# Two empty steps in the context lane of the gate/up stage, and its first step ahead of the weave

## The chip, the cores and the metric

One core of a Trainium2 chip runs the kernel. Its engines work side by side, each through a list of instructions in order: TensorE (PE: products and transposes), VectorE (DVE), ScalarE (ACT), GpSimd (POOL), and SyncE (SP), which only issues loads. They wait for each other on semaphores. The metric is the time of one execution on the chip, in microseconds, as the median of several runs.

## The reference

The kernel computes two blocks of a transformer in a row on `x` (256 tokens of 1024), in float32. The first block is a hybrid attention mixer followed by a gated feed-forward. The second is a gated linear attention (GLA) and retention mixer, started from states that a context of 256 further tokens yields, followed by experts that choose their tokens. Cut to what the changed loop computes:

```python
def _swiglu(h, w_gate_up, w_down):
    gate, up = jnp.split(h @ w_gate_up, 2, axis=-1)      # 22 weight slots
    return (jax.nn.silu(gate) * up) @ w_down

hc = _rmsnorm(ctx, norm1_w[i]) * (1.0 + mod_c[1]) + mod_c[0]
def _context_states(hc, w_in, gla_gate_w, gla_gate_b, ret_decay_logit):
    _, gk, gv, log_a, _, _, rk, rv, _ = _project(hc, w_in, gla_gate_w, gla_gate_b, None)
    # log_a = log_sigmoid(z @ gla_gate_w + gla_gate_b) / 16
    log_gamma = jax.nn.log_sigmoid(ret_decay_logit.astype(F32))
    s_gf = _gla_final_state(gk, gv, log_a[:, :, 0])      # k * exp(b_end - b), then k^T v
    s_gb = _gla_final_state(_flip(gk), _flip(gv), _flip(log_a[:, :, 1]))
    s_rf = _ret_final_state(rk, rv, log_gamma[0])
    s_rb = _ret_final_state(_flip(rk), _flip(rv), log_gamma[1])
    return (s_gf, s_gb, s_rf, s_rb)
```

The feed-forward of the first block (gate/up, then down) and the context's states of the second do not depend on each other.

## The kernel before

All activations stay on the chip; the weights come as slots of 128 x 2048 numbers (1 MB) into a ring, in the order of the list `ORDER`, and `sync` issues a slot's load when the last user of its place is done. A dense product (`dense`, L656 to L658) runs at reduced precision in three passes per weight tile, with weights and activations split in a high and a low part. ScalarE copies a slot to its high part (`top_half`, L2404), VectorE subtracts for the low part (`low`, L1490), then TensorE makes 24 products over both token tiles; ScalarE and VectorE prepare slot n+2 while TensorE is at slot n.

The stage of the change is the gate/up product. It is woven from three lanes, Python generators of which each `yield` ends a step:

- "g" (`ffn` in each engine, 23 steps): slot n of gate/up. A group of 256 features is complete after two slots; then ScalarE takes a tanh (L2597), VectorE forms the gated product (L1367, called for it in its `ffn`), and with the next even slot TensorE transposes it (`gated_T`, L565 through `tr`), behind that slot's products. ScalarE copies the transposes out (L2587) ahead of its next copy of a slot.
- "c" (`context` in each engine, 22 steps): first the setup: ScalarE issues the loads of the context and its gates' weights, and a small log-sigmoid of 8 numbers per row is taken (VectorE L1367, ScalarE L2603 and L2605, VectorE L1367). Then the context's norm: squares (L2363), reciprocal root on GpSimd (L2857, L2859), scaling by VectorE (L1453) and ScalarE (L2365), eight tiles transposed by TensorE in four steps (L565) and copied out with scale and shift (L1463, L2375). Then three projection slots (`proj`, L957), the gates' narrow product z (L967), `pre` (L975), the log-sigmoid of 128 x 1024 (L1943, L1367, ScalarE L2603, L2605, VectorE L1367, L1946), decay products (L987, L989) with exp (L2640) and key scaling (L1952), state products (L1001), projection slots 3 to 6, scaling of the retention keys (L1972, L1977), and the last state products in two pairs (L1020), of which each bank is copied out (L1984 by VectorE, L2653 by ScalarE) before it is used again.
- "f" (VectorE alone, 20 steps): half a slot of the modulation weights each (`vads`, L1409).

`schedules` makes one list of letters, `FFN`, that TensorE, VectorE, ScalarE and the order of the loads go through alike: at a letter, an engine runs the next step of that lane (an engine that has no "f" skips it). No lane's step is tied to another's by the weave here: it takes "g f c f" in turn until each lane is used up:

```python
n = {"g": 23, "c": 22, "f": 2 * len(UNITS_FFN)}
ffn = weave(dict.fromkeys(n, 0), n, {}, "gcf", "gfcf")
```

So c_k stands behind g_k, all through. An engine's own list is rigid: where an instruction waits, all behind it wait. The list also orders the loads: a gate/up slot at each "g", the slots of the context's weights at given steps of "c". Before the loop stands the end of the attention block (`post`, `norm_scaled`, L635); behind it the down projection, whose first two slots are prepared by ScalarE and VectorE in the steps g_20 and g_21.

Of the kernel before, what the change touches and what calls it, by code (L numbers as in the profile page):

```python
# [52 lines left out]
def weave(done, counts, needs, main, turns):  # L53

    out = []
    while any(done[k] < counts[k] for k in main):
        for k in turns:
            if done[k] < counts[k] and all(done[a] >= n for a, n in needs.get((k, done[k]), ())):
                out.append(k)
                done[k] += 1  # L60
    return out


def schedules():

    n = {"p": 3, "f": 16, "0": 18, "1": 18, "i": 24, "d": 7, "c": 14, "o": 7}
    done = dict.fromkeys(n, 0)
    att = weave(done, n, {}, "p", "pf")
    needs = {}
    for h in "01":  # L70
        for t in range(2):
            needs[h, 12 + 3 * t] = [("d", 7), ("i", 12 * (t + 1))]
    for t in range(2):
        needs["c", 9 + 4 * t] = [("0", 3 * t + 3), ("1", 3 * t + 3)]
    for k in range(2):
        needs["o", k] = [("i", 12)]
    needs["o", 2] = [("0", 12), ("1", 12), ("c", 14), ("i", 21)]
    att += weave(done, n, needs, "0i1dco", "icf0i1do")
    att += "f" * (n["f"] - done["f"])
    n = {"g": 23, "c": 22, "f": 2 * len(UNITS_FFN)}  # L80
    ffn = weave(dict.fromkeys(n, 0), n, {}, "gcf", "gfcf")
    return att, ffn


# [1 line left out]
UNITS_IN1, UNITS_OUT1, UNITS_FFN, UNITS_DN = list(range(8, 18)), [18, 19], [20, 21, 22, 23] + list(range(32, 38)), list(range(38, 48))  # L86
# [85 lines left out]
class Book:  # L172
# [11 lines left out]
    def sig(self, name, *index):  # L184
        engine, lane, *event = name.split()
        key = f"{engine}_{lane}"
        if key not in self.sems:
            self.sems[key] = self.make(f"s_{key}")
        n = self.count[key] = self.count.get(key, 0) + 1
        if event:  # L190
            if self.dry:
                assert (name, *index) not in self.value, (name, index)
                self.value[(name, *index)] = n
            assert self.value[(name, *index)] == n, (name, index)
        self.latest[engine] = (self.sems[key], n)
        return self.sems[key], 1
# [48 lines left out]
def build(nc, D, out, coff):  # L245

    ctx = ExitStack()
    with ctx:
# [38 lines left out]
        def two(v):  # L287
            return v.rearrange("p (t d) -> p t d", t=2)
# [149 lines left out]
        seen = {"f": 0, "c": 0, "u": 0, "g": 0}  # L438
# [12 lines left out]
        for k in FFN:  # L451
            if k == "g" and seen["g"] < len(PLAN["gu"]):
                want_dense("gu", seen["g"])
            if k == "c" and seen["c"] in (6, 7, 8, 15, 16, 17, 18):
                i = (6, 7, 8, 15, 16, 17, 18).index(seen["c"])
                g, k0, kk = PLAN_CTX[i]
                n = kk * G_CTX[g][1]
                want("ctx", i, D["w_ctx"][i][:, 0:n], n)
            if k == "f" and seen["f"] % 2 == 0:
                want_vad(UNITS_FFN[seen["f"] // 2])  # L460
            seen[k] += 1
# [97 lines left out]
        def tensor(e):  # L559
# [38 lines left out]

            def norm(S, junk, banks, free):

                yield
                for k in range(0, 8, 2):
                    b = banks[k // 2 % len(banks)]
                    w.wait_ge(*at(f"v {S} x0"))
                    w.wait_ge(*at(f"a {S} x1"))
                    for f in free(k):
                        w.wait_ge(*f)
                    for j in (k, k + 1):
                        for t in range(2):
                            i = tr(PS[:, b, 256 * (j % 2) + 128 * t:256 * (j % 2) + 128 * t + 128], two(junk)[:, t, 128 * j:128 * j + 128])  # L610
                    i.then_inc(*sig(f"pe {S} tr", k))
                    yield
# [324 lines left out]
            def context():  # L937
# [28 lines left out]
                for k in range(8):  # L966
                    i = mm(PS[0:32, 7, 0:256], GZW[:, k, :], hcv[:, k, :], start=k == 0, stop=k == 7)  # L967
# [4 lines left out]
                for t in range(2):  # L972
                    if t:
                        w.wait_ge(*at("v ctx ev", 1))
                    mm(PS[:, 7 - t, :], GZc[0:32, 128 * t:128 * t + 128], GWc[0:32, :], start=True, stop=True).then_inc(*sig("pe ctx pre", t))  # L975
                yield
                L, KW = two(CX[:, 0:1024]), CX[:, 1024:2048].rearrange("p (d t n) -> p d t n", d=2, t=2)
                for d in range(2):
                    for t in range(2):
# [7 lines left out]
                        i = mm(PS[:, b, 0:256], C("gt") if d == 0 else C("lt"), L[:, t, 256 * d:256 * d + 256], start=True, stop=not far)  # L987
                        if far:
                            i = mm(PS[:, b, 0:256], C("ones"), L[:, 1 - t, 256 * d:256 * d + 256], start=False, stop=True)  # L989
                        i.then_inc(*sig("pe ctx kw", d, t))  # L990
                    yield
                for d in range(2):
                    for r in range(2):
# [6 lines left out]
                        for t in range(2):  # L1000
                            i = mm(PS[:, 7 - r, 0:256], KW[:, d, t, 128 * r:128 * r + 128], pcv[:, t, 256 + 256 * r:512 + 256 * r], start=t == 0, stop=t == 1)  # L1001
# [297 lines left out]
            n = 0  # L1299
# [62 lines left out]
        def vector(e):  # L1362
# [87 lines left out]
            def norm(S, src, junk, st, banks, aff, dst, mine=(2, 6)):  # L1450

                w.wait_ge(*at(f"g {S} rs"))
                ts(two(junk)[:, 0, :], src[:, 0, :], st[:, 2:3], None, ALU.mult).then_inc(*sig(f"v {S} x0"))  # L1453
                yield
                for k in range(0, 8, 2):
                    if k in mine:
                        b = banks[k // 2 % len(banks)]
                        w.wait_ge(*at(f"pe {S} tr", k))
                        if aff is None:
                            cp(dst[:, 256 * k:256 * k + 512], PS[:, b, :]).then_inc(*sig(f"v {S} h", k))  # L1460
                        else:
                            for j in (k, k + 1):
                                i = ts(dst[:, 256 * j:256 * j + 256], PS[:, b, 256 * (j % 2):256 * (j % 2) + 256], aff[:, j:j + 1], aff[:, 8 + j:9 + j], ALU.mult, ALU.add)  # L1463
                            i.then_inc(*sig(f"v {S} h", k))
                    yield
# [452 lines left out]
            def context():  # L1918
# [26 lines left out]
                chain()  # L1945
                ts(CX[:, 0:1024], CX[:, 0:1024], 1.0 / 16.0, None, ALU.mult).then_inc(*sig("v ctx L"))  # L1946
                yield
                for d in range(2):
                    for t in range(2):
                        w.wait_ge(*at("a ctx kw", d, t))  # L1950
                        w.wait_ge(*at("a ctx ev", 0))
                        tt(KW[:, d, t, :], KW[:, d, t, :], pcv[:, t, 0:256], ALU.mult).then_inc(*sig("v ctx kw", d, t))  # L1952
                    yield
# [354 lines left out]
            n = 0  # L2308
# [23 lines left out]
        def scalar(e):  # L2332
# [25 lines left out]
            def norm(S, src, junk, st, banks, aff, dst, free=(), mine=(0, 4)):  # L2358

                for f in free:  # L2360
                    w.wait_ge(*f)
                for t in range(2):
                    act(two(junk)[:, t, :], src[:, t, :], ACT.Square, scale=1.0 / 32, accum_out=st[:, t:t + 1]).then_inc(*sig(f"a {S} sq", t))  # L2363
                w.wait_ge(*at(f"g {S} rs"))
                act(two(junk)[:, 1, :], src[:, 1, :], ACT.Identity, scale=st[:, 3:4]).then_inc(*sig(f"a {S} x1"))  # L2365
                yield
                for k in range(0, 8, 2):
                    if k in mine:
                        b = banks[k // 2 % len(banks)]
                        w.wait_ge(*at(f"pe {S} tr", k))  # L2370
                        if aff is None:
                            act(dst[:, 256 * k:256 * k + 512], PS[:, b, :], ACT.Copy).then_inc(*sig(f"a {S} h", k))
                        else:
                            for j in (k, k + 1):
                                i = act(dst[:, 256 * j:256 * j + 256], PS[:, b, 256 * (j % 2):256 * (j % 2) + 256], ACT.Identity,  # L2375
                                        scale=aff[:, j:j + 1], bias=aff[:, 8 + j:9 + j])
                            i.then_inc(*sig(f"a {S} h", k))
                    yield
# [222 lines left out]
            def log_sigmoid(S, u):  # L2601
                w.wait_ge(*at(f"v {S} abs"))
                act(u, u, ACT.Exp, scale=-1.0).then_inc(*sig(f"a {S} exp"))  # L2603
                chain()
                act(u, u, ACT.Ln, bias=1.0).then_inc(*sig(f"a {S} ln"))  # L2605

            def context():
# [24 lines left out]
                    yield  # L2632
                yield
                log_sigmoid("ctxg", CX[:, 1024:2048])
                yield
                KW = CX[:, 1024:2048].rearrange("p (d t n) -> p d t n", d=2, t=2)
                for d in range(2):
# [193 lines left out]
            n = 0  # L2831
# [213 lines left out]
```

## Time and profile before

| | |
|---|---|
| median of 3 runs | 1363.94 us (1363.89 to 1365.08) |
| the profiled execution | 1366.02 us, its span 1364.2 us |
| PE busy | 1015.9 us, 74% |
| DVE busy | 527.0 us, 39% |
| ACT busy | 290.9 us, 21% |
| mean granted TensorE clock | 0.867 of full |

The gate/up stage lies at about 270 to 477 us of the span. Times in the views are us from the start of the span, and L numbers are lines of the kernel before. A timeline row gives start, duration, engine, line, what is written and read, the count of instructions merged, and in brackets how long the engine had been idle and what ended that. A line may be that of a helper that many steps call, so it is told apart by its time. Most of the 1.0 to 2.3 us rows on DVE and ACT in this stage are splits of weight slots.

### The profile page before, as it was taken

The numbers are of one execution on the slowest core, as the hardware profiler recorded it, in microseconds if no ns is written. First come the engines' busy times: TensorE is split into PE (matmuls) and PEld (weight loads), VectorE is DVE, ScalarE is ACT, GpSimd is POOL, SyncE is SP. The second block draws the span as 40 slices with busy tenths as digits, with TensorE's granted clock in tenths as the row PEclk, the third lists the DMA queues.
The fourth block names the chain that finished last, engine by engine and source line by source line (L and its number), as shares of the span: only waits on it lengthen the run. The fifth ranks groups of instructions, "written<-read, shape, count | busy, mean of one in ns | idle before, by whom it ended". The sixth has DMA issues, their size and how long they took to land.

```text
span 1364.2 us, 13077 instructions
## 1 busy us (share of the span) xinstructions
PE 1015.9 (74%) x5454; PEld 587.7 (43%) x5454; DVE 527.0 (39%) x1001; ACT 290.9 (21%) x465; POOL 25.4 (2%) x38
## 2 busy tenths in 40 slices
PE   1797888899989998999987866555555655566594
PEld 0575667777675786777864311111111111111131
DVE  6876667686553498577674100000000000000001
ACT  3322244452241333551332100000000000000000
POOL 0000000000000000000000000000000000000000
PEclk9997788899989999899987866777787788877878
DMA  9896211567634468232359999999999999999996
GB/s 387 329 376 242 95 62 62 193 253 275 249 120 154 157 253 343 79 135 89 115 209 420 425 429 431 431 431 428 432 430 430 431 428 432 431 430 431 429 431 264
DMA packets 41147, 415.16 MB, mean 304 GB/s; under 512 B 4928, under 2 KB 4928, under 8 KB 7808
## 3 DMA queue, kind: packets, MB, share of 16 engines
q1 hardware_dynamic: 38304, 405.75, 72.6%
q10 hardware_dynamic: 2784, 8.57, 1.7%
q8 instruction: 43, 0.70, 0.2%
q14 instruction: 16, 0.13, 0.0%
HBM read 413.26 MB, written 1.05 MB: 304 GB/s over the span
## 4 chain that ended last, share of the span: by engine, by line
PE 42%; DMA 41%; DVE 12%; ACT 3%; issue 2%; POOL 1%; DVEq 0%; SPq 0%
DMA ring<-in_w_egu 26%; DMA ring<-in_w_ed 10%; PE PS L656 7%; PE PS L657 7%; PE PS L658 7%; PE PS L957 4%; PE PS L1274 3%; DVE ringR L1490 2%; DMA arena<-in_w_ed 2%; PE PS L565 2%; PE PS L1336 2%; DMA ring<-in_w_in 1%; DVE arena L1367 1%; ACT ringR L2404 1%; DVE ring L1409 1%
## 5 line engine op out<-in xcount | busy, mean ns | idle before, releaser
L1274 PE MATMUL PS<-ring,arena 128*32 128x512 f32 (+1 forms) x1152 | 179.9, 761 | 100.0 <-DMA ring<-in_w_egu 99.7
L656 PE MATMUL PS<-ringR,arenaR 128*128 128x512 f32 (+1 forms) x520 | 215.2, 414 | 24.0 <-DVE arenaR L1478 23.5
L657 PE MATMUL PS<-ringR,arenaR 128*128 128x512 f32 (+1 forms) x520 | 207.4, 399 | 0.0
L658 PE MATMUL PS<-ringR,arenaR 128*128 128x512 f32 (+1 forms) x520 | 207.2, 398 | 0.0
L1490 DVE TENSOR_TENSOR ringR<-ring,ringR 128x2048 fp32r<-128x2048 f32 (+1 forms) x66 | 148.7, 2254 | 98.7 <-ACT ringR L2404 98.6
L1367 DVE SCALAR_TENSOR_TENSOR arena<-arena,PS 128x256 f32<-128x256 f32 (+2 forms) x68 | 33.2, 498 | 368.0 <-ACT arena L2837 360.9
L2404 ACT ACTIVATE ringR<-ring 128x2048 fp32r<-128x2048 f32 (+1 forms) x66 | 123.9, 1885 | 88.7 <-PE PS L658 54.0
L1274 PEld LDWEIGHTS PS<-ring,arena 128*32 128x32 f32 x1152 | 36.8, 131 | 233.4 <-DMA ring<-in_w_egu 171.2
L1336 PE MATMUL PS<-ring,arena 128*32 128x512 f32 x512 | 82.9, 782 | 59.5 <-DMA ring<-in_w_ed 58.9
L656 PEld LDWEIGHTS PS<-ringR,arenaR 128*128 128x128 f32 x520 | 99.5, 191 | 51.0 <-DVE arenaR L1478 24.4
L2837 ACT ACTIVATE arena<-PS 128x512 f32<-128x512 f32 (+1 forms) x12 | 6.7, 561 | 503.0 <-PE PS L1274 503.0
L657 PEld LDWEIGHTS PS<-ringR,arenaR 128*128 128x128 f32 x520 | 99.7, 192 | 23.5 <-issue 1.4
L658 PEld LDWEIGHTS PS<-ringR,arenaR 128*128 128x128 f32 x520 | 99.3, 191 | 23.7
L565 PE MATMUL PS<-CT,arena 128*128 128x128 f32 (+2 forms) x304 | 52.5, 317 | 67.6 <-DVE arena L1367 26.7
L1409 DVE CUSTOM_DVE_ANT_0 ring<-ring 128x1024 f32<-128x1024 f32 x80 | 94.8, 1219 | 0.3 <-DVE ring L1438 0.2
L2323 DVE TENSOR_TENSOR arena<-PS,arena 128x512 f32<-128x512 f32 x8 | 5.2, 688 | 209.1 <-PE PS L1336 209.1
L1274 PE MATMUL PS<-arena 128*32 128x512 f32 (+1 forms) x384 | 56.9, 724 | 32.4 <-DMA arena<-in_w_egu 32.4
L565 PEld LDWEIGHTS PS<-CT,arena 128*128 128x128 f32 (+2 forms) x304 | 40.9, 163 | 91.2 <-DVE arena L1367 41.2
L1336 PEld LDWEIGHTS PS<-ring,arena 128*32 128x32 f32 x512 | 16.0, 126 | 122.6 <-DMA ring<-in_w_ed 91.3
L957 PE MATMUL PS<-ring,arena 128*128 128x512 f32 (+1 forms) x128 | 49.3, 539 | 1.5 <-DVE arena L1463 1.5
L1336 PE MATMUL PS<-arena 128*32 128x512 f32 x192 | 30.6, 771 | 17.8 <-DMA arena<-in_w_ed 17.8
L1274 PEld LDWEIGHTS PS<-arena 128*32 128x32 f32 x384 | 12.1, 127 | 72.5 <-DMA arena<-in_w_egu 51.8
(344 smaller groups left out, 887.9 us busy)
## 6 DMA issues: line engine op xcount, KB each, us to landing
ring<-in_w_egu SPq DMA_DIRECT2D x48, 2048.0 KB, 35.5
ring<-in_w_ed SPq DMA_DIRECT2D x32, 2048.0 KB, 34.4
ring<-in_w_vad SPq DMA_DIRECT2D x40, 1024.0 KB, 7.0
ring<-in_w_egu SPq DMA_DIRECT2D x24, 1536.0 KB, 29.6
arena<-in_w_egu SPq DMA_DIRECT2D x16, 2048.0 KB, 35.2
ring<-in_w_in SPq DMA_DIRECT2D x22, 1024.0 KB, 4.8
ring<-in_w_gu SPq DMA_DIRECT2D x22, 1024.0 KB, 4.9
arena<-in_w_ed SPq DMA_DIRECT2D x11, 2048.0 KB, 32.5
```

The costliest lines, as they stand in the source:

```text
L565: return e.transpose(o, i, ident[0:k, 0:k])
L656: mm(o, xh(k, t), hi[:, c], start=k == 0, stop=False)
L657: mm(o, xh(k, t), s.viewr[:, c], start=False, stop=False)
L658: i = mm(o, xl(k, t), hi[:, c], start=False, stop=k == nk - 1)
L957: i = mm(PS[:, 5 + t, 0:wc], hcv[:, k, 128 * t:128 * t + 128], s.view[:, (k - k0) * wc:(k - k0 + 1) * wc], start=k == 0, stop=k == 7)
L1274: i = mm(PS[32 * ee:32 * ee + 32, b + a_, 0:fw], XEv[:, k, grp, 32 * ee:32 * ee + 32], wv[:, ee, a_, :], start=k == 0, stop=k == 7, tile_p ...
L1336: i = mm(PS[32 * ee:32 * ee + 32, 6 + hh, :], HT[:, 128 * c + 32 * ee:128 * c + 32 * ee + 32], wv[:, 512 * ee:512 * ee + 512], start=c == ...
L1367: return e.scalar_tensor_tensor(out=o, in0=a, scalar=s, in1=b, op0=o0, op1=o1)
L1409: i = e.tensor_tensor_reduce(out=wv, in0=wv, in1=CB[:, 1024 * b:1024 * b + 1024], scale=1.0, scalar=0.0, op0=ALU.mult, op1=ALU.add, accum_ ...
L1490: tt(s.viewr, s.view, high(S, n), ALU.subtract).then_inc(*sig(f"v {S} lo", n))
L2404: act(high(S, n), s.view, ACT.Copy).then_inc(*sig(f"a {S} hi", n))
L2837: act(TA[:, 512 * (n % 2):512 * (n % 2) + fw], PS[:, 2 * (n % 2), 0:fw], ACT.Tanh, scale=0.5).then_inc(*sig("a moe ta", n))
```

## The change

The context lane gets two more steps without work on every engine: one behind the norm's scaling (in each engine's `norm`; the start's norm uses the same function and ignores empty steps), one behind the gates' log-sigmoid. Its count goes from 22 to 24, and its first step is put ahead of the list, so that from then on c_k stands behind g_(k-1). The steps at which the context's weights are asked for are renumbered to stay with their projections.

```diff
--- before.py
+++ after.py
@@ -77,8 +77,8 @@
     needs["o", 2] = [("0", 12), ("1", 12), ("c", 14), ("i", 21)]
     att += weave(done, n, needs, "0i1dco", "icf0i1do")
     att += "f" * (n["f"] - done["f"])
-    n = {"g": 23, "c": 22, "f": 2 * len(UNITS_FFN)}
-    ffn = weave(dict.fromkeys(n, 0), n, {}, "gcf", "gfcf")
+    n = {"g": 23, "c": 24, "f": 2 * len(UNITS_FFN)}
+    ffn = ["c"] + weave({"g": 0, "c": 1, "f": 0}, n, {}, "gcf", "gfcf")
     return att, ffn
 
 
@@ -451,8 +451,8 @@
         for k in FFN:
             if k == "g" and seen["g"] < len(PLAN["gu"]):
                 want_dense("gu", seen["g"])
-            if k == "c" and seen["c"] in (6, 7, 8, 15, 16, 17, 18):
-                i = (6, 7, 8, 15, 16, 17, 18).index(seen["c"])
+            if k == "c" and seen["c"] in (7, 8, 9, 17, 18, 19, 20):
+                i = (7, 8, 9, 17, 18, 19, 20).index(seen["c"])
                 g, k0, kk = PLAN_CTX[i]
                 n = kk * G_CTX[g][1]
                 want("ctx", i, D["w_ctx"][i][:, 0:n], n)
@@ -598,6 +598,7 @@
 
             def norm(S, junk, banks, free):
 
+                yield
                 yield
                 for k in range(0, 8, 2):
                     b = banks[k // 2 % len(banks)]
@@ -974,6 +975,7 @@
                         w.wait_ge(*at("v ctx ev", 1))
                     mm(PS[:, 7 - t, :], GZc[0:32, 128 * t:128 * t + 128], GWc[0:32, :], start=True, stop=True).then_inc(*sig("pe ctx pre", t))
                 yield
+                yield
                 L, KW = two(CX[:, 0:1024]), CX[:, 1024:2048].rearrange("p (d t n) -> p d t n", d=2, t=2)
                 for d in range(2):
                     for t in range(2):
@@ -1451,6 +1453,7 @@
 
                 w.wait_ge(*at(f"g {S} rs"))
                 ts(two(junk)[:, 0, :], src[:, 0, :], st[:, 2:3], None, ALU.mult).then_inc(*sig(f"v {S} x0"))
+                yield
                 yield
                 for k in range(0, 8, 2):
                     if k in mine:
@@ -1945,6 +1948,7 @@
                 chain()
                 ts(CX[:, 0:1024], CX[:, 0:1024], 1.0 / 16.0, None, ALU.mult).then_inc(*sig("v ctx L"))
                 yield
+                yield
                 for d in range(2):
                     for t in range(2):
                         w.wait_ge(*at("a ctx kw", d, t))
@@ -2364,6 +2368,7 @@
                 w.wait_ge(*at(f"g {S} rs"))
                 act(two(junk)[:, 1, :], src[:, 1, :], ACT.Identity, scale=st[:, 3:4]).then_inc(*sig(f"a {S} x1"))
                 yield
+                yield
                 for k in range(0, 8, 2):
                     if k in mine:
                         b = banks[k // 2 % len(banks)]
@@ -2632,6 +2637,7 @@
                     yield
                 yield
                 log_sigmoid("ctxg", CX[:, 1024:2048])
+                yield
                 yield
                 KW = CX[:, 1024:2048].rearrange("p (d t n) -> p d t n", d=2, t=2)
                 for d in range(2):
```

In `tensor`, the two empty steps stand ahead of the norm's transposes and behind `pre`; in `scalar` and `vector`, behind the scaling and behind the log-sigmoid.

## Rows read from the trace of the kernel before

**Rows 1.** The page, part 4: the chain that ended last, share of the span by engine.

```profile
PE 42%; DMA 41%; DVE 12%; ACT 3%; issue 2%; POOL 1%; DVEq 0%; SPq 0%
```

**Rows 2.** Waits of TensorE, 255 to 600 us: who waited <- for whom: us, times, longest.

```profile
PE PS L987 <- DVE arena L1946: 6.3, 1, 6.3
...
PE PS L957 <- DVE arena L1463: 1.5, 1, 1.5
```

**Rows 3.** Loads issued from 250 to 480 us: queue, count, KB, median us to landing.

```profile
arena<-in_rows ACTq DMA_DIRECT2D x1, 4.0 KB, 2.6
```

**Rows 4.** Timeline of VectorE, 276 to 284 us: start, duration, instruction [idle before <-releaser].

```profile
276.61 2.29 DVE L1490 TENSOR_TENSOR ringR<-ring,ringR 128x2048 fp32r<-128x2048 f32 x1
...
280.15 0.17 DVE L1367 SCALAR_TENSOR_TENSOR arena<-arena 128x8 f32<-128x8 f32 x1
...
283.99 2.29 DVE L1490 TENSOR_TENSOR ringR<-ring,ringR 128x2048 fp32r<-128x2048 f32 x1 [0.56 <-ACT ringR L2404]
```

**Rows 5.** Timeline of ScalarE, 280 to 292 us.

```profile
280.58 1.28 ACT L2605 ACT_TABLE_LOAD   x1
...
281.99 1.90 ACT L2404 ACTIVATE ringR<-ring 128x2048 fp32r<-128x2048 f32 x1
...
285.74 1.06 ACT L2363 ACTIVATE arena<-arena 128x1024 f32<-128x1024 f32 x1
...
289.92 1.15 ACT L2365 ACTIVATE arena<-arena 128x1024 f32<-128x1024 f32 x1 [1.99 <-POOL arena L2859]
...
291.45 1.90 ACT L2404 ACTIVATE ringR<-ring 128x2048 fp32r<-128x2048 f32 x1
```

**Rows 6.** Timeline of TensorE, 281 to 292 us.

```profile
281.90 0.40 PE L656 MATMUL PS<-ringR,arenaR 128*128 128x512 f32 x1
...
288.00 0.63 PE L565 MATMUL PS<-CT,arena 128*128 128x128 f32 x4 [0.35 <-DVE arena L1367]
291.21 0.63 PE L565 MATMUL PS<-CT,arena 128*128 128x128 f32 x4 [2.58 <-ACT arena L2365]
```

**Rows 7.** Timeline of TensorE at 380 us.

```profile
379.89 1.22 PE L987 MATMUL PS<-arena,CT 128*128 128x256 f32 x2 [6.28 <-DVE arena L1946]
```

**Rows 8.** Timeline of VectorE, 368 to 380 us.

```profile
368.45 2.29 DVE L1490 TENSOR_TENSOR ringR<-ring,ringR 128x2048 fp32r<-128x2048 f32 x1 [7.17 <-ACT ringR L2404]
...
379.75 2.29 DVE L1490 TENSOR_TENSOR ringR<-ring,ringR 128x2048 fp32r<-128x2048 f32 x1
```

**Rows 9.** Stretches: bounds, length, PE busy (count), granted clock, DMA share, GB/s.

```profile
288.60:291.20 2.60, 0.03 (x1) 1.00 0.52 217
378.00:384.90 6.90, 5.01 (x12) 0.51 0.00 1
545.30:552.10 6.80, 5.99 (x28) 0.50 0.00 0
689.70:695.50 5.80, 5.76 (x14) 0.50 0.00 0
```

**Rows 10.** Timeline of VectorE, 463 to 476 us.

```profile
463.78 0.17 DVE L1972 TENSOR_SCALAR arena<-arena 128x16 f32<-128x16 f32 x1
464.05 2.49 DVE L1977 TENSOR_TENSOR arena<-arena 128x512 f32<-128x512 f32 x4
471.10 2.29 DVE L1490 TENSOR_TENSOR ringR<-ring,ringR 128x2048 fp32r<-128x2048 f32 x1 [4.56 <-ACT ringR L2404]
473.31 0.42 DVE L1984 COPY arena<-PS 128x256 f32<-128x256 f32 x1
...
475.85 1.72 DVE L1367 SCALAR_TENSOR_TENSOR arena<-arena,PS 128x256 f32<-128x256 f32 x4
```

**Rows 11.** Timeline of TensorE, 470 to 478 us.

```profile
470.11 0.48 PE L656 MATMUL PS<-ringR,arenaR 128*128 128x512 f32 x1
...
475.79 1.95 PE L1020 MATMUL PS<-arena 128*128 128x128 f32 x16
477.49 0.48 PE L656 MATMUL PS<-ringR,arenaR 128*128 128x512 f32 x1
```

## The prediction, made before the change was run

> **What bounds the kernel now.** I read the chain of the page first: it goes over PE for 42% and over DMA for 41%, the transfers being the expert weights of the last stage [rows 1]. A stage that waits for its own bytes ends later or earlier with its start, so whatever the gate/up stage far ahead of it wins or loses should pass on at its full size. I then asked whom TensorE waits for from 255 to 600 us, around the changed loop. In the loop it has two large waits and a smaller one: 6.3 us at L987 (the context's first decay product, for the log-sigmoid's scaling at L1946), 2.6 us at L565 for ScalarE's L2365 (the context norm's second scaling), 1.5 us at L957 (first projection) for L1463 [rows 2, 6]. Otherwise its queue is full, so in this loop the order of TensorE's list and what stands late against it decide.
>
> **What the lists become.** A lane step c_k stands behind g_k before. After, c_0 stands ahead of g_0 and c_k behind g_(k-1). With one empty step in the norm, its transposes keep their place behind g_2 to g_5, and so do the first three projections, z and pre; but the setup (was behind g_0) is now ahead of g_0, and squares and scaling (was behind g_1) stand behind g_0. With the second empty step all that follows the log-sigmoid stands one g later: decay products behind g_12 and g_13, projections 3 to 6 behind g_16 to g_19, the key scaling (L1972, L1977) on VectorE behind g_20 (was g_19), the last products L1020 behind g_21 and g_22 (were g_20, g_21). g_22 is an empty step on each engine. On SP's queue the weights of projections 3 to 6 come one gate/up load later; they are asked for as far ahead as now, so I cost that at nothing. Without the cover the price would be one landing, some 5 us (the 2.6 us of a 4 KB row [rows 3] is its lower bound).
>
> **Part A, the front.** Before, VectorE's split of weight slot 2 starts at 276.61, and the small log-sigmoid comes at 280.15 [rows 4]. After, the log-sigmoid comes first, at about 276.75; its row was asked for at 269.8 and lands in 2.6 us [rows 3]. From its start to ScalarE's next copy it took 1.84 us (280.15 to 281.99, with a table load inside [rows 4, 5]). So ScalarE's copy of slot 2 starts at 278.6 and takes 1.9 us, and VectorE's split takes 2.3 us behind it: 280.6 to 282.9. TensorE is due for slot 2 at 281.90 [rows 6]: it waits 1.0 us. Next the squares and scalings: from the squares' start to that of L2365 it was 285.74 to 289.92, 4.18 us with GpSimd between, and 1.15 more for L2365 itself [rows 5]. They start at 280.4, so L2365 ends at 285.7. Behind it ScalarE copies slot 3 (to 287.5), VectorE splits it from 287.63, and the gate products L1367 follow; from split start to the transposes that need them it was 283.99 to 288.00, 4.01 us [rows 4, 6]. So these transposes start at 291.64, and the norm's some 0.4 us behind at 292.04, with no wait for L2365 any more, against 291.21 before [rows 6]: **+0.8** for TensorE. The wait for L2365 goes; the gate products are late in its place. ScalarE is later by more: its copy of slot 4 can start when the transposes are copied out, at 292.78 against 291.45 [rows 5], +1.33, and this reaches TensorE at L957, which already waits 1.5 us for VectorE [rows 2]. **A = +1.3 us** (0.8 if that chain has slack, 2.5 if the granted clock falls in the new 2.9 us gap).
>
> The clause that weighs here is the table load: it now lies on the path to slot 2. The row shows 1.28 us (280.58 to 281.86) and the next copy 0.13 us behind it [rows 5]. The Trainium skill (ScalarE: Activation LUTs, What ACT_TABLE_LOAD costs) adds a drain of 1.38 us to each switch, about 2.66 us in all. By that page the wait at slot 2 would be 2.4 us and the whole sum below larger by 1.4 us, by estimate. The trace has no room for such a gap behind this load.
>
> **Part B, the log-sigmoid.** TensorE's slot 11 ends at 379.89 - 6.28 = 373.61 [rows 7]. After, slot 12 stands in this gap; its split starts at 368.45 and takes 2.3 us [rows 8], in time. With A it runs from 374.94 for 5.68 us (slot 21: 470.11 to 475.79 [rows 11]) to 380.62. But behind slot 12 stands the transpose of group 5, and that needs gate products that VectorE makes behind the scaling L1946 and behind the split of slot 13: 379.75 + 1.33 = 381.08 [rows 8], plus the 4.01 us of part A = 385.1. So TensorE waits 4.5 us in place of 6.3: **-1.8 us**. The wait is not removed; most of it turns into one for L1367.
>
> The clock: half (1.2 GHz) was granted from 378.0 to 384.9, 4.4 us after work had ended at 373.61, and 5.0 us of work fell into it [rows 9], which at 2.4 GHz takes 2.5: 2.5 us lost. In the gap of 2.6 us before 291.2 the clock stayed full [rows 9]. The new 4.5 us gap lies between these. Half may be granted late in it or not at all; the stretches at half lasted 6.8 to 6.9 us [rows 9], so the loss lies between 0 and 3.4 us. I take 1.6, half of such a stretch being busy. **Clock = -2.5 + 1.6 = -0.9 us** (-2.5 to +0.9).
>
> **Part C, the tail.** Before, the key scaling ran in VectorE's idle time behind g_19, from 463.78 to 464.05 + 2.49 = 466.54; the split of down slot 0 came at 471.10 [rows 10]. After, it is queued behind that split: from 473.31 for 2.76 us to 476.07. TensorE: with the first L1020 pair no longer between g_20 and g_21, slot 21 starts 1.78 us earlier, at 468.33, and ends at 474.01; then L1020 wants the scaled keys and waits until 476.15, **2.14 us**. A pair takes 1.70 us (475.79 to 477.49 [rows 11]), to 477.85. The second pair needs bank 5 copied out by VectorE, and that copy stands behind the split of down slot 1 (2.21 us, as 471.10 to 473.31) and the last gate products (1.64 us of the 1.72): it runs from 479.85 for 0.42 us to 480.27 [rows 10]. TensorE waits until 480.35, **2.50 us**; the second pair ends at 482.05, where the down projection starts, against 477.49 [rows 11]. **C = +4.56 us.** These waits are new: both pairs now stand behind the last slot, with no TensorE work between them. They hold at any shift from A and B, since ScalarE and VectorE follow TensorE's transposes here.
>
> **Sum.** +1.3 - 1.8 - 0.9 + 4.56 = **+3.1 us**, rounded. The profiled execution took 1366.02 us (span 1364.2) and gives 1369.1; it lay 2.08 us above the median of the three runs, on which I expect 1363.94 + 3.1 = **1367.0 us**. Further back the stretches at half clock can fall otherwise against the shifted work; I put 0 there, within 1.5 us both ways.
>
> **The rivals.**
> 1. The same mechanisms, each at its small end: A +0.8, clock -2.5, 1 us won from a later half-clock stretch: 0.8 - 1.8 - 2.5 + 4.56 - 1 = 0, so 1364.0, and from there to 1366.6. For it: the clock term alone spans 3.4 us. Against: it wants several lucky ends. 37%.
> 2. Faster, by the granted clock alone: full clock is kept through the 4.5 us gap, and the shifted stages behind meet less of the half clock. In two of the later stretches 6.0 + 5.8 us of TensorE work run at half [rows 9], so up to 5.9 us can come back. With full clock at 380 us the sum is +1.3 - 1.8 - 2.5 + 4.56 = +1.5; it decides from 4.2 us returned, and at 5.0 the time is 1360.4. For it: the stretches are long. Against: the gaps that cause them stay. 7%.
> 3. Slower by more: half clock also after the new gaps of A and C, 1.7 us each, and 0.9 more in B: 3.1 + 4.3 = +7.4, 1371.3. For it: these gaps come in pairs close together. Against: the 2.6 us gap kept its clock. 8%.
> 4. The change does not do what it says: the wait for L2365 stays. Its squares start 5.3 us earlier, so I give it no chance of its own; the time would be that of rival 1.
>
> **How the numbers follow.** Forecast 48%, rivals 37, 7 and 8%. A difference can be told from no change at about 0.2%, 2.7 us. Slower takes rival 3 and nearly all of the forecast: 0.54. Faster 0.07, same 0.39. The range leaves out the ends of rivals 2 and 3: 1362.6 to 1370.4; the forecast's own is 1366.6 to 1369.5.
>
> **What would show it.** Right: the wait of L987 for L1946 gone, and one of some 4.5 us at L565 for L1367 near 385 us; the wait for L2365 gone, about 3 us for L1367 near 291 us and 1 us at L656 for L1490 near 282 us; two waits at L1020 of 2.1 and 2.5 us near 475 and 479 us, for L1977 and L1984. Wrong: no wait at L1020 and the down projection starting before 479 us, or ScalarE waiting for a gate/up load behind 350 us.

## The result, and the profile after

The changed kernel takes 1371.53 us (median of 20 runs, 1370.1 to 1373.76) against 1364.78 us of the kernel before (20 runs): 6.75 us slower, ratio 1.005, interval 1.0042 to 1.0058. The direction was forecast, the size was not: 3.1 us were, and the range ended at 1370.4. Of the 4.5 us between the forecast of 1367.0 and 1371.53, 0.84 us are the base: the forecast stood on the median of three runs, 1363.94.

The changed kernel's profiled execution took 1370.10 us (span 1368.3 us). Its page, the chain that ended last; line numbers have moved by up to 6 (L656 is L657, L987 is L989, L1020 is L1022, L1367 is L1369, L1977 is L1981, L1984 is L1988):

```profile
PE 43%; DMA 39%; DVE 12%; ACT 3%; issue 2%; POOL 1%; DVEq 0%; SPq 0%
```

Waits of TensorE in it, 255 to 490 us, the answer to [rows 2] (who waited <- for whom: us, times, longest):

```profile
PE PS L565 <- DVE arena L1369: 7.5, 2, 4.6
...
PE PS L1022 <- DVE arena L1988: 2.1, 1, 2.1
PE PS L1022 <- DVE arena L1981: 2.0, 1, 2.0
PE PS L657 <- DVE ringR L1493: 0.9, 1, 0.9
PE PS L958 <- DVE arena L1466: 0.7, 1, 0.7
```

Each wait that the prediction named is there. The 6.3 us at the decay products are gone and 4.6 us stand at the transposes; the 2.6 us for L2365 are gone and 7.5 - 4.6 = 2.9 us stand for the gate products; 0.9 us for slot 2; and the two waits of the tail, 2.0 and 2.1 us. What the forecast missed is not in this view, since it is no wait. TensorE's timeline of the tail (rows that answer to [rows 11]):

```profile
473.12 2.05 PE L1022 MATMUL PS<-arena 128*128 128x128 f32 x16 [1.97 <-DVE arena L1981]
...
477.30 2.56 PE L1022 MATMUL PS<-arena 128*128 128x128 f32 x16 [2.13 <-DVE arena L1988]
479.51 0.77 PE L657 MATMUL PS<-ringR,arenaR 128*128 128x512 f32 x1
...
486.35 0.60 PE L565 MATMUL PS<-CT,arena 128*128 128x128 f32 x4
```

The second pair needs 477.30 to 479.51 = 2.21 us from start to start where it took 1.70, and the first down slot 6.84 us (to 486.35). Stretches of the changed kernel (bounds, length, PE busy, granted clock, DMA share, GB/s):

```profile
290.50:297.80 7.30, 7.30 (x28) 0.77 0.74 288
383.30:393.40 10.10, 10.03 (x41) 0.84 0.00 1
471.20:479.50 8.30, 4.25 (x32) 0.95 0.36 128
479.50:486.40 6.90, 6.90 (x27) 0.81 0.38 133
704.30:717.20 12.90, 12.90 (x52) 0.88 0.91 362
```

and those of the kernel before that answer to the last two:

```profile
477.50:483.20 5.70, 5.70 (x28) 1.00 0.81 327
700.10:711.60 11.50, 11.50 (x53) 1.00 0.91 360
```

The first down slot is the same work: 6.9 us at a mean of 0.81 against 5.7 at 1.00. And far behind the change, in the second block's last projection, 12.9 us at 0.88 against 11.5 at 1.00. So stretches at half clock (1.2 GHz) stand right behind the new waits, and one stands far behind them where before had none.

### The profile page after: what moved, and what is told of

Read it like the earlier page. It is cut to its first block, busy times and chain, and to the rows that moved or that the text cites. A ratio compares the mean times of both kernels' runs of the same rounds, so it can differ in the third digit from the quotient of the medians.

```text
span 1368.3 us, 13077 instructions
## 1 busy us (share of the span) xinstructions
PE 1014.1 (74%) x5454; PEld 587.3 (43%) x5454; DVE 527.2 (39%) x1001; ACT 291.6 (21%) x465; POOL 25.5 (2%) x38
## 4 chain that ended last, share of the span: by engine, by line
PE 43%; DMA 39%; DVE 12%; ACT 3%; issue 2%; POOL 1%; DVEq 0%; SPq 0%
DMA ring<-in_w_egu 22%; DMA ring<-in_w_ed 12%; PE PS L657 7%; PE PS L659 7%; PE PS L658 7%; PE PS L1276 4%; PE PS L958 4%; PE PS L565 2%; DVE ringR L1493 2%; DMA arena<-in_w_ed 2%; DVE arena L1369 1%; DMA ring<-in_w_in 1%; PE PS L1338 1%; ACT ringR L2409 1%; PE PS L1254 1%
## 5 line engine op out<-in xcount | busy, mean ns | idle before, releaser
L1276 PE MATMUL PS<-ring,arena 128*32 128x512 f32 (+1 forms) x1152 | 175.4, 746 | 103.5 <-DMA ring<-in_w_egu 103.2
L657 PE MATMUL PS<-ringR,arenaR 128*128 128x512 f32 (+1 forms) x520 | 216.0, 415 | 26.8 <-DVE arenaR L1481 23.7
L1369 DVE SCALAR_TENSOR_TENSOR arena<-arena,PS 128x256 f32<-128x256 f32 (+2 forms) x68 | 33.2, 497 | 370.5 <-ACT arena L2843 360.6
L1338 PE MATMUL PS<-ring,arena 128*32 128x512 f32 x512 | 86.9, 812 | 54.3 <-DMA ring<-in_w_ed 53.8
L657 PEld LDWEIGHTS PS<-ringR,arenaR 128*128 128x128 f32 x520 | 100.6, 193 | 54.2 <-DVE arenaR L1481 24.6
```

The lines of the kernel that those rows point to most:

```text
L657: mm(o, xh(k, t), hi[:, c], start=k == 0, stop=False)
L1276: i = mm(PS[32 * ee:32 * ee + 32, b + a_, 0:fw], XEv[:, k, grp, 32 * ee:32 * ee + 32], wv[:, ee, a_, :], start=k == 0, stop=k == 7, tile_p ...
L1338: i = mm(PS[32 * ee:32 * ee + 32, 6 + hh, :], HT[:, 128 * c + 32 * ee:128 * c + 32 * ee + 32], wv[:, 512 * ee:512 * ee + 512], start=c == ...
L1369: return e.scalar_tensor_tensor(out=o, in0=a, scalar=s, in1=b, op0=o0, op1=o1)
```

## The experiments

The kernel before ran beside each set; its medians there were 1364.53 (e1 to e4), 1364.67 (e5 to e8), 1364.28 (e9 to e12) and 1365.13 us (e13 to e16).

### The three parts by themselves (e1 to e4)

**e1_front**, part A alone:

```diff
+    n = {"g": 23, "c": 23, "f": 2 * len(UNITS_FFN)}
+    ffn = ["c"] + weave({"g": 0, "c": 1, "f": 0}, n, {}, "gcf", "gfcf")
     # norm: second yield as in the change; none behind the log-sigmoid
```

> Part A alone: the norm's empty step and the first step ahead, no empty step at the log-sigmoid, the end of the lane where it was. Theory (waits as in the changed kernel, plus half clock that new short waits bring): waits of about 1 us for the split of slot 2 and 2.9 us for the first gate products, together +1.3 us at the first projection, +0 to 2 us of clock; total +1 to +3 us. Rival (part A costs most of the 6.7 us by what it does to the phase of all that follows): +4 us or more. Rival 2 (A gains, as the wait for the second scaling goes): below 0.

Measured 1365.28 us, +0.75, interval 0.9986 to 1.0017. TensorE is 0.9 us late at the down projection. That is just below what was expected. The rival of +4 us falls by the time; the interval leaves room for a small gain, which only the trace speaks against.

**e2_lsig**, part B alone, without a tail:

```diff
+    n = {"g": 23, "c": 23, "f": 2 * len(UNITS_FFN)}
+    ffn = weave(dict.fromkeys(n, 0), n, {}, "gcf", "gfcf")
+    last = len(ffn) - 1 - ffn[::-1].index("c")
+    del ffn[last]
+    at_g = [i for i, k in enumerate(ffn) if k == "g"][20]
+    ffn.insert(at_g, "c")
     # yield behind the log-sigmoid as in the change; none in norm
```

> Part B alone: the empty step behind the log-sigmoid, no change at the front, and the two steps ahead of the last products (the last projection's, the key scaling's) taken in one go behind g_19, so that the last products stand where they stood before. Theory: one wait of 4.6 us at the transposes near 383 us in place of 6.3 us at the decay products, no waits at the last products: -1.8 us of wait and up to -2.5 us of clock, total -1.5 to -4 us. Rival (the second empty step is of itself a loss): 0 or more.

Measured 1364.93 us, interval 0.9997 to 1.0057 (three of the twelve runs lay 12 us and more above the rest). The wait is as foretold (4.6 us), and TensorE is 2.0 us ahead at the down projection; the time is level. A miss by the time: the gain is made and does not arrive. More on this below.

**e3_tail**, part C alone:

```diff
     ffn = weave(dict.fromkeys(n, 0), n, {}, "gcf", "gfcf")
+    c19 = [i for i, k in enumerate(ffn) if k == "c"][19]
+    del ffn[c19]
+    ffn.append("c")
```

> Part C alone: no empty step anywhere, only the last three steps of the context lane each stand one g later than before (key scaling behind g_20, last products behind g_21 and g_22). Theory: two waits of 2.0 and 2.1 to 2.5 us at the last products, +4.1 to 4.6 us, and 1.7 us of half clock on them and on the first down slot: +5 to +7 us in all, nearly the whole loss. Rival (forecast as it was written, no clock loss): +4.6 us. Rival 2 (the down projection absorbs it): under +2 us.

Measured 1372.41 us, +7.9, interval 1.0042 to 1.0068. The last products in it, each with its wait:

```profile
476.42 3.37 PE L1023 MATMUL PS<-arena 128*128 128x128 f32 x16 [1.97 <-DVE arena L1980]
480.61 2.05 PE L1023 MATMUL PS<-arena 128*128 128x128 f32 x16 [0.81 <-DVE arena L1987]
```

and the stretch over the tail:

```profile
474.50:482.40 7.90, 5.16 (x32) 0.78 0.40 135
```

The tail by itself gives the whole loss, a little more than the 5 to 7 us expected. Here half clock falls on the first pair, already behind the first wait; the pair then takes up most of the second wait, the first down slot runs at full clock (5.6 us), and the down projection starts 4.95 us late all the same. Both the rival of 4.6 us and that of an absorbed delay fall.

**e4_both**, the changed kernel without its tail (the three lines of e2 that move a "c" ahead of g_20, in the changed kernel):

> The changed kernel with only its tail taken back: both empty steps, first step ahead, but the last projection's and the key scaling's step in one go behind g_19, so the last products stand behind g_20 and g_21 as before. Theory: A + B = +1.6 - 2.8 = -1 us, -3 to +1 us; the waits at the last products gone. Rival (the loss comes from A or from B): +3 us or more remain.

Measured 1364.67 us, +0.1, interval 0.9994 to 1.0011. As expected: the loss goes with the tail.

### What the tail costs beyond its waits (e5, e6)

**e5_filler**, unused work in the two waits of the changed kernel:

```diff
                 for h in range(4):
-                    w.wait_ge(*at("v ctx rk"))
                     w.wait_ge(*at("v ctx ev", 3))
                     w.wait_ge(*at("a ctx ev", 3))
+                    if h % 2 == 0:
+                        for _ in range(2):
+                            mm(PS[:, 6, :], hcv[:, 0, 0:128], hc[:, 0:512], start=True, stop=True)
+                    w.wait_ge(*at("v ctx rk"))
```

> The changed kernel with two extra products of 128x512 (0.86 us each, results not used) put into each of the two waits of the tail, ahead of the wait for the scaled keys and ahead of the third product. Nothing else is changed. Theory (about 1.7 us of the tail is half clock that these waits bring): the first down slot takes 5.7 us again instead of 6.8, the waits shrink by the filler, the down projection starts no later; total 1 to 2 us below the changed kernel (1371.5), near 1370. Rival (the tail is its waits alone and the rest of the loss comes from elsewhere): as the changed kernel, 1371 to 1372.

Measured 1368.78 us, 2.75 below the changed kernel's 1371.53 (another set), interval to before 1.0012 to 1.0037. Tail, then most of the first down slot:

```profile
471.90:480.20 8.30, 7.63 (x42) 1.00 0.35 128
480.20:485.60 5.40, 5.40 (x25) 1.00 0.51 170
```

TensorE is idle for 0.7 us instead of 4.1, the down projection starts no earlier than in the changed kernel (+4.26 us against +4.03), the clock stays at 2.4 GHz, the first down slot takes 5.63 us instead of 6.84, and the kernel with more work is faster. This shows the half clock as a term of its own. The 2.75 us are above the 1 to 2 us expected, but not all of them are the tail's: in the traces e5 is 1.0 us ahead of the changed kernel at the second block's first norm, and 1.2 us more come behind it.

**e6_bank**, one wait of the tail taken away (TensorE's side; VectorE's copy reads bank 6 for the third product, and a later wait is set to that copy):

```diff
-                    b = 7 if h % 2 else 5
-                    if h > 1:
-                        w.wait_ge(*at("a ctx sr" if h % 2 else "v ctx sr", h - 2))
+                    b = 7 if h % 2 else 5 + h // 2
+                    if h > 1 and h % 2:
+                        w.wait_ge(*at("a ctx sr", h - 2))
```

> The changed kernel with the third of the last four products in bank 6, which is free by then, instead of in bank 5, which has to be copied out first. Theory: the second wait of the tail (2.1 us) goes, the first (2.0 us) stays; with less idle time less half clock: 2 to 3.5 us below the changed kernel, 1368 to 1369.5. Rival (VectorE's late copies hold the down projection in any case): 1371 to 1372.

Measured 1364.47 us, level with before (interval 0.9984 to 1.0021) and 7.1 us below the changed kernel. Both pairs stand behind its one wait in the tail:

```profile
474.56 3.84 PE L1022 MATMUL PS<-arena 128*128 128x128 f32 x32 [1.97 <-DVE arena L1981]
```

A miss by size: one wait of 2.1 us was worth 7. Counted from the norm ahead of the stage (the section on why says how), TensorE reaches the down projection after 218.24 us in the changed kernel and 215.32 here, 2.9 us less; 1.2 more go with the first down slot's half clock, and 3 between the second block's first norm and the third expert load. The profiled execution took 1370.49 us, 6 above the median: its last stage, from the third expert load on, ran 3.7 us longer than that of any other trace, so this trace is used up to the third load alone.

### Moving the small log-sigmoid (e7, e8, e13)

```diff
                 load("gateb", GBrc, row("gateb"))
-                log_sigmoid("ctxl", ul)
                 yield
                 w.wait_ge(*at("v nc affine"))
-                yield from norm("nc", CXv, pc, stc, (5, 6, 7), affs2[:, 32:48], hc, [loaded("ctx")])
+                steps = norm("nc", CXv, pc, stc, (5, 6, 7), affs2[:, 32:48], hc, [loaded("ctx")])
+                next(steps)
+                yield
+                log_sigmoid("ctxl", ul)
+                yield from steps
```

and the same on VectorE. **e7_best** has it on e4_both, **e8_front2** on e1_front, **e13_best_again** is e7 once more.

> The changed kernel with the tail taken back as in e4_both, and with the small log-sigmoid moved out of the first step into the norm's empty step on VectorE and ScalarE, so that it no longer stands ahead of weight slot 2. Theory (part A's waits of 1 and 2.9 us come from the small log-sigmoid ahead of slot 2): both gone, as well as the old 2.6 us wait for the second scaling; 1.5 to 4 us below e4_both and before, 1360.5 to 1363. Rival (the gate products are late because of squares and scaling, not of the log-sigmoid): a wait of 1 to 3 us near 289 us stays, 1364 to 1365.

> Only the front: the norm's empty step, the first step ahead, and the small log-sigmoid in that empty step; nothing at the log-sigmoid of the gates, tail as before. Theory: 2 to 3 us below before through the front alone, 1361.5 to 1363, the 6.3 us wait at the decay products stays. Rival (a wait that goes here is given back at the first projection, which waits for a gate/up load): within 1 us of before.

> e7_best once more, for a second set of times: its trace had TensorE 3.4 us ahead of before at the second block's first norm and 2.4 us ahead at the end, its median of 12 was level. Theory (what is won ahead of the norm is lost behind it): 1364 to 1365.5. Rival (the first set was unlucky): 1361 to 1363.

Measured: e7 1365.23 us (+0.6, interval 0.9974 to 1.0021), e8 1365.31 us (+0.6, interval 0.9995 to 1.0045), e13 1364.66 us (-0.5, interval 0.9957 to 1.0016). Waits of TensorE in e7, 275 to 500 us:

```profile
PE PS L569 <- DVE arena L1373: 6.1, 3, 4.6
PE PS L962 <- DVE arena L1470: 1.5, 1, 1.5
...
PE PS L661 <- DVE ringR L1497: 0.7, 1, 0.7
```

e7 and e8 miss what was expected by the time; e13, level once more, is as expected. The 2.9 us for the gate products have shrunk to at most 1.5, but 0.7 us for slot 2 stay (squares and scaling now stand ahead of ScalarE's copy of it), and so do the 1.5 us at L962 (L957 of before), which had been 0.7 us in the changed kernel. By this move TensorE is earlier at the first projection by 1.95 us (e8 against e1) and 2.6 us (e7 against e4), and at the down projection by 1.1 and 2.4 us. So the small log-sigmoid ahead of slot 2 is more than the 1.57 us that part A costs, and without it the front gains only 0.4 us there. In e8 TensorE is just 0.2 us ahead at the down projection, which is what its rival said. The lead of e7 and e13, 3.4 us at the down projection, stands in both traces and does not arrive in the medians. (Their profiled executions, 1371.87 and 1371.5 us, lie 7 us above the medians and came to this stage 8 us later than that of before; the counting below takes that out.)

### Pure delays (e9 to e12)

k products without use on TensorE ahead of the down projection of the kernel before, k = 2, 4, 6; **e12_after_again** is the changed kernel:

```diff
+            w.wait_ge(*at("v ctx ev", 3))
+            for _ in range(k):
+                mm(PS[:, 6, :], ident, CT[:, 0:512], start=True, stop=True)
             gh = [tile(rnd(mods2)), tile(rnd(GUH))]
```

> The kernel before with 2 extra products of 128x512 (0.86 us each, results not used) on TensorE between the last products of the context and the down projection: a pure delay of about 1.7 us there, without a wait. Theory (stages behind, which run partly at half clock, turn a small shift into almost nothing and a shift of 4 us and more into 6 to 8): +0 to +1 us at the end, 1364 to 1365.5. Rival (a shift passes on at its size): +1.7 us, 1366.3.

> The same with 4 extra products, a pure delay of about 3.4 us. Theory (a step, not a line): either still under +1.5 or already +5 and more, or runs that fall into both; not all near +3.4. Rival: +3.4 us, 1368.0.

> The same with 6 extra products, a pure delay of about 5.2 us, about what the tail alone (e3_tail) brought at the down projection. Theory: +6.5 to +8 us, 1371 to 1372.5, as for e3_tail, though nothing waits in the tail. Rival: +5.2 us, 1369.8.

> The changed kernel unaltered, beside the delays on the same chip, and for a second look at its clock. Theory: 1371 to 1372, the first down slot and the products of the second block's last projection again partly at half clock. Rival (the half clock on the first down slot was that one execution's): 5.7 us for this slot, and waits as before.

Measured 1367.40, 1368.06, 1370.33 and 1371.61 us: +3.1, +3.8, +6.0 and +7.3 (intervals 1.0014 to 1.0032, 1.0018 to 1.0035, 1.0028 to 1.0052, 1.0036 to 1.006). My theory of a step falls: the smallest delay passes on with more than its size, and the middle one with its size; the largest, +6.0 for 5.2, lies between theory and rival. e12 repeats the changed kernel's trace within 0.2 us up to the third load; the first down slot again takes 6.8 us, at a mean clock of 0.83.

### Keeping the clock in the gap (e14 to e16)

**e15_before_full** (kernel before, 7 products) and, with 5 products ahead of `gated_T` at n == 12, **e14_lsig_full** on e2_lsig and **e16_best_full** on e7_best:

```diff
+                w.wait_ge(*at("v ctx pre", 1))
+                for _ in range(7):
+                    mm(PS[:, 7, :], ident, CT[:, 0:512], start=True, stop=True)
                 for d in range(2):
                     for t in range(2):
                         w.wait_ge(*at("v ctx L"))
```

> e2_lsig (the log-sigmoid's empty step alone, tail taken back) with 5 extra products of 128x512 (0.86 us each, unused) in the 4.6 us gap behind slot 12, so that TensorE keeps full clock there. Theory of part B (1.8 us of wait and 2.5 us of clock to be had): TensorE about 4.3 us ahead at the down projection. If gains pass on: 1360 to 1361. If they are lost behind the norm, as for e2_lsig: 1363.5 to 1365.

> The kernel before with 7 extra products in its 6.3 us gap ahead of the first decay product, nothing else. Measures the half clock there by itself: 2.5 us ahead at the down projection. If gains pass on: 1362. If they are lost behind: 1363.5 to 1365.

> e13 with the 5 extra products of e14 in its gap: all that was won in the gate/up stage together, about 5.5 us ahead at the down projection. If a loss of 5 us here becomes 7, a gain of 5 us should reach another step: 1358 to 1361. If every gain is lost behind: 1363.5 to 1365.

Measured: e14 1361.55 us (interval 0.9943 to 0.9989, without one run of 1382.22), e15 1361.62 us (0.9956 to 1.0016, with one run of 1379.88 in it), e16 1362.98 us (0.9957 to 1.0003). e15 is as expected, e14 half a microsecond above, e16 between its two cases. The gap and what follows it in e15:

```profile
370.90:377.20 6.30, 6.03 (x15) 1.00 0.49 168
377.20:385.70 8.50, 8.50 (x40) 1.00 0.05 8
```

The clock is full through the gap. From the first decay product to slot 13 (slot 12 and the second decay products lie between) the kernel before took 379.89 to 390.76 = 10.9 us; here it is 8.5 us, since none of it runs at half clock. By medians e14 and e15 are 3.5 us below before and 10 below the changed kernel; e15's interval still includes no change, e14's does not. The lead does pass on here, which speaks against "every gain is lost behind the norm"; the largest lead, e16's, does not give the best time.

## Why the prediction was wrong

To compare traces in which this part starts up to 11 us apart, I count from the start of the products of the norm ahead of the stage (L635: 263.28 before, L636: 261.27 after). Shifts against before, in us: at the start of the down projection, at the second block's first norm (the next L635 block), at the third expert load (711.64 before, 717.25 after), and in the medians, each against before's median of its own set. The last column is not a shift but the time from that norm to the third load:

```
                 down    norm   third load   median   norm to load
before           0       0          0          0       165.53
after           +4.03   +5.21      +7.62      +6.75   167.94
e12 (again)     +4.11   +5.20      +7.52      +7.3    167.84
e3  tail        +4.95   +5.01      +7.32      +7.9    167.83
e11 delay 5.2   +5.15   +5.52      +6.78      +6.0    166.79
e5  filler      +4.26   +4.24      +5.46      +4.1    166.75
e10 delay 3.4   +3.08   +3.40      +3.42      +3.8    165.56
e9  delay 1.7   +1.34   +1.71      +4.00      +3.1    167.82
e6  bank        +1.11   +1.16      +0.62      -0.2    164.98
e1  front       +0.90   +0.90      +0.50      +0.75   165.13
e8  front2      -0.20   -0.19      -0.12      +0.6    165.61
e4  both        -1.04   -1.04      +0.16      +0.1    166.74
e2  lsig        -2.01   -2.01      +0.47      +0.4    168.01
e15 before full -2.41   -2.42      -2.83      -3.5    165.12
e7  best        -3.43   -3.43      -0.97      +0.6    167.99
e13 best again  -3.39   -3.39      -0.94      -0.5    167.98
e14 lsig full   -4.31   -4.32      -3.29      -3.6    166.56
e16 best full   -4.54   -4.54      -3.36      -2.15   166.71
```

- **Part A** was +1.3; at slot 11 the trace has +1.57. Waits of 0.94 and 2.90 us (1.0 and 2.9 forecast), so the table load that now lies ahead of slot 2 added no more than its 1.28 us. Right within 0.3 us, but not in all its terms: half clock fell behind the second wait (slot 3: 290.57 to 297.80 = 7.2 us, 1.6 more than before), which the +1.3 did not have, and the first projection's wait shrank from 1.5 to 0.7 us and hid half of it.
- **Part B** was -1.8 - 0.9 = -2.7; from slot 11 to slot 14 the trace has 1.57 to -1.19 = -2.76, with the steps taken out that stand at another slot now: the wait of 4.6 us (4.5 forecast), the clock loss near 1.6 (10.1 us at 0.84). Right in the trace. e2 has the same wait alone; e14 and e15 give back the half clock.
- **Part C** was +4.56, named in place and order, and is the step that failed by size: it had no clock term. To the down projection the trace has 4.03 + 1.19 = +5.22 (5.07 against e4, which lacks only the tail): waits of 4.10 us (4.64 forecast), 0.5 us of half clock on the second pair, and 0.5 us since the last products before a wait count with their whole duration (0.39 us against a spacing of 0.23 us in slot 21, the first pair 2.05 against 1.70). The first down slot adds 1.19 us of half clock (6.84 against 5.65). So C is **+6.4 us**. The clock term was written down, but as rival 3 with 8% and not in the sum. e5 shows that it is real: with the waits filled and the down projection as late, TensorE is 1.0 us earlier at the next norm.
- **"I put 0 there"** for what lies behind was the second error. From the norm to the third load the changed kernel loses 2.4 us more, the last 1.3 of them between first and third load (12.55 against 11.26 us, and 0.88 against 1.00 of clock in the rows above), repeated in e12. The last stage, which waits for the expert weights, then runs 651.0 to 653.2 us in every trace but e6's (656.9); in the changed kernel's it is 1.5 us shorter than in that of before (651.0 against 652.6).
- **The sum** adds up to +3.16, not +3.1, which changes nothing. With what was measured it is 1.57 - 2.76 + 6.4 + 2.4 = +7.6 at the third load, and +6.75 in the medians.

Rival 1 asked for lucky ends in A and B, and there were none. Rival 2's mechanism, the clock alone, is seen in e15 (2.4 us ahead at the down projection with nothing but unused products), but not in this change. Rival 3 is nearest in the number, 1371.3, and that is in part luck: of its 4.3 us only the 1.7 us of C came as priced. A's half clock came (1.6 us) but left only 0.3 us above the forecast, B's 0.9 us did not come, and the 2.4 us further back are not in it. Rival 4 falls: the wait for L2365 is gone.

**Where the shifts change behind the norm.** The medians follow the shift at the third load within 1.6 us in all rows, the shift at the norm only within 4.1. Between the two lies the same work in all traces, and it takes 165.0 to 168.0 us. The last column falls into four narrow groups: 165.0 to 165.1 (e1, e6, e15), 165.5 to 165.6 (before, e8, e10), 166.6 to 166.8 (e4, e5, e11, e14, e16) and 167.8 to 168.0 (the changed kernel and e12, e2, e3, e7, e9, e13). In each group the stretches at half clock lie, counted from that norm, in the same places within 0.6 us. In the seven traces of the last group, and in no other, one of them lies between the first and the third load, and that part takes 12.5 to 12.6 us instead of 11.3. So 2.4 us of the changed kernel's loss, and 2.5 us of the lead of e7, are the step from the group of before to the slowest one, while e14 goes to the third group and keeps 3.3 of its 4.3 us.

**What stays open.** The group doesn't follow the size of the shift: the slowest has traces 3.4 us ahead and 5.2 us late at the norm, that of before one 3.4 us late. What decides it is not shown, and no run held the clock in that stretch, so that the half clock is the cause there is argued from where it lies. The two kernels that were profiled twice (the changed kernel and e12, e7 and e13) fell into the same group both times, but how often other executions do is not known.

## What to carry to other kernels

An empty step that moves one lane against the others moves all of its later steps too: follow the lane to its end, and look above all at where the cover runs out, because the last steps pile up behind the last slot; taking the moved steps up again ahead of it (e4) removed the whole loss. Count a new idle gap of 2 us and more on TensorE as the gap plus a half clock that it may bring (1.7 us for the tail here, 1.6 us on slot 3), and put that into the sum as a term, even where one trace shows a gap without it. A gap that can't be closed can be filled with unused products: in the kernel before that put TensorE 2.4 us ahead and the median 3.5 us lower.

## What the runs showed of the hardware that I had not expected

- Whether a wait of 2 to 3 us brings half clock isn't told by its length. The wait of 2.6 us for the norm's scaling stands in eight traces (before, e2, e3, e9, e10, e11, e14, e15); half clock came behind it in two, e3 and e11, and not in the other six. A single wait of 1.97 us in the tail brought it in e3 and did not in e6, whose first down slot took 5.63 us. The stretch behind the 2.6 us wait, before and in e3 (PE busy, granted clock):

```profile
291.20:297.60 6.40, 6.39 (x32) 1.00 0.69 269
```

```profile
291.10:297.60 6.50, 6.42 (x23) 0.74 0.72 268
```

- More work was faster twice: 4 unused products in the tail gave 2.75 us back (e5), 7 in the gap 3.5 us by the medians, with an interval that still includes no change (e15).
- A pure delay of 1.7 us on TensorE cost 3.1 us at the end (e9), one of 3.4 us cost 3.8 (e10). Their times from the norm to the third load, 167.8 and 165.6 us, go with that.
